# Three norms' rows turned by products with a diagonal, two early GpSimd steps, fewer idle products, and one wait moved, in a kernel of three transformer blocks

## The reference, cut to what matters

```python
def rmsnorm(x, g):
    y = x * lax.rsqrt(jnp.mean(x * x, axis=-1, keepdims=True) + EPS)
    return y * g

h = x                                               # block 1
h = h + token_mixer(rmsnorm(h, norm_mix), ...)      # two kinds of attention
h = h + hierarchical_moe(rmsnorm(h, norm_ffn), ...) # 32 experts of width 512
# blocks 2 and 3, l = 0 and 1
m = silu(c) @ w_ada[l] + b_ada[l]                   # six vectors: shifts, scales, gates
x = x + g_m * mixer(modulate(x, ...))               # l=0: attention with a context and a Fourier part; l=1: convolution
x = x + g_f * ec_moe(modulate(x, ...))              # 16 experts of width 1024, 32 rows each
```

## Time and profile before

| what | value |
|---|---|
| median of 3 runs | 1843.66 us (1841.27 to 1847.12) |
| the profiled execution, its own time | 1841.28 us |
| its span, first to last instruction | 1839.4 us |
| TensorE, VectorE, ScalarE, GpSimd busy | 77%, 27%, 13%, 5% of the span |
| data moved | 719 MB, 391 GB/s on average |
| first block's mixer | 0 to about 184 us |
| first mixture of experts | to about 640 us |
| second block's mixer | to about 830 us |
| its experts | to about 1260 us |
| third block's mixer | to about 1405 us |
| its experts and the end | to 1839.4 us |

### The profile page before, as it was taken

How to read it: one execution, slowest core, us unless ns; L and a number is a source line. 1 busy time by engine, 2 the same in 40 slices (tenths; PEclk the granted TensorE clock), 3 DMA queues, 4 the chain that set the end, 5 groups by cost and what they waited for, 6 DMA issues and landing times.

```text
span 1839.4 us, 30498 instructions
## 1 busy us (share of the span) xinstructions
PE 1419.1 (77%) x13602; PEld 818.7 (45%) x13602; DVE 488.9 (27%) x999; ACT 246.0 (13%) x561; POOL 83.1 (5%) x92
## 2 busy tenths in 40 slices
PE   9999886676588999999566666668999756666675
PEld 5456443333244454666233334326866433333332
DVE  5874221111221169841000000004643100000000
ACT  3233211111211113411000000001001000000000
POOL 3100000000000042100000000000000000000000
PEclk9999988888899999999777768789999877878888
DMA  9775999999999996788999999999998999999997
GB/s 366 261 291 236 386 428 427 426 427 425 426 421 422 402 340 245 296 355 368 431 431 429 430 431 431 426 427 390 392 379 332 429 432 432 428 431 431 431 423 323
DMA packets 79232, 719.28 MB, mean 391 GB/s; under 512 B 5104, under 2 KB 11000, under 8 KB 49656
## 3 DMA queue, kind: packets, MB, share of 16 engines
q1 hardware_dynamic: 76336, 712.85, 93.3%
q10 hardware_dynamic: 2760, 4.40, 0.7%
HBM read 716.18 MB, written 1.06 MB: 390 GB/s over the span
## 4 chain that ended last, share of the span: by engine, by line
DMA 50%; PE 38%; DVE 6%; issue 2%; POOL 2%; ACT 1%; SPq 0%; ACTq 0%; DVEq 0%
DMA ring<-in_moe_w_down 33%; PE bank L1792 9%; DMA ring<-in_w_down 8%; PE bank L2685 5%; PE bank L535 3%; DMA ring<-in_attn_w_in 3%; PE bank L1734 3%; DMA ring<-in_moe_w_gate 2%; PE bank L1743 2%; PE bank L1047 2%; PE bank L1016 2%; PE bank L679 2%; DMA room<-in_rows 1%; PE bank L2445 1%; PE bank L1646 1%
## 5 line engine op out<-in xcount | busy, mean ns | idle before, releaser
L1743 PE MATMUL bank<-ring,arena 128*32 128x256 f32 x3840 | 284.4, 460 | 165.4 <-DMA ring<-in_moe_w_up 123.6
L1792 PE MATMUL bank<-ring,arena 128*32 128x256 f32 x2944 | 236.1, 482 | 143.0 <-DMA ring<-in_moe_w_down 115.9
L1743 PEld LDWEIGHTS bank<-ring,arena 128*32 128x32 f32 x3840 | 159.1, 131 | 286.7 <-issue 219.7
L1792 PEld LDWEIGHTS bank<-ring,arena 128*32 128x32 f32 x2944 | 122.1, 136 | 244.8 <-issue 193.6
L1734 PE MATMUL bank<-ring,arena 128*32 128x512 f32 x976 | 130.5, 656 | 61.2 <-ACT arena L1834 32.0
L1865 DVE TENSOR_TENSOR arena<-arena,bank 128x128 f32<-128x128 f32 (+1 forms) x64 | 22.7, 354 | 503.9 <-PE bank L1743 496.5
L535 PE MATMUL bank<-ring,low 128*128 128x512 f32 (+1 forms) x352 | 150.9, 576 | 0.1
L1820 PE MATMUL bank<-arena 32*128 32x256 f32 x1024 | 92.6, 431 | 15.1 <-PE bank L1820 10.6
L1876 ACT ACTIVATE arena<-bank 128x256 f32<-128x256 f32 x64 | 24.6, 385 | 560.3 <-PE bank L1806 558.2
L535 PEld LDWEIGHTS bank<-ring,low 128*128 128x128 f32 x352 | 64.4, 190 | 64.3 <-issue 63.4
L1734 PEld LDWEIGHTS bank<-ring,arena 128*32 128x32 f32 x976 | 27.3, 114 | 140.3 <-issue 60.3
(11 more groups left out here) (322 smaller groups left out, 1336.5 us busy)
## 6 DMA issues: line engine op xcount, KB each, us to landing
ring<-in_moe_w_gate SPq DMA_DIRECT2D x20, 4096.0 KB, 24.4
ring<-in_moe_w_up SPq DMA_DIRECT2D x20, 4096.0 KB, 23.6
ring<-in_moe_w_down SPq DMA_DIRECT2D x20, 4096.0 KB, 23.7
ring<-in_w_gate SPq DMA_DIRECT2D x31, 2048.0 KB, 22.4
ring<-in_w_up SPq DMA_DIRECT2D x30, 2048.0 KB, 23.6
ring<-in_w_down SPq DMA_DIRECT2D x30, 2048.0 KB, 24.5
ring<-in_ada_w SPq DMA_DIRECT2D x24, 2048.0 KB, 13.7
ring<-in_moe_w_up SPq DMA_DIRECT2D x22, 2048.0 KB, 20.7
```

The source lines that it names most:

```text
L1743: last = nc.tensor.matmul(GU[up][32 * j:32 * j + 32, 0:QW], xgT[:, x + kk, a:a + C], w[:, kq, j * QW:(j + 1) * QW], start=(kk == 0), stop= ...
L1792: last = nc.tensor.matmul(z_bank(M)[32 * j:32 * j + 32, 0:QW], act_s[:, kk, :], w[:, kq, j * QW:(j + 1) * QW], start=(kk == 0), stop=(kk = ...
```

## The change

Four edits are made together.

- In the norms 0, 2 and 4 the rows are not scaled any more. ScalarE and VectorE scale the 128x128 identity by the roots instead, into the first 128 columns of the tile that held the squares, and `tr_pe` multiplies each raw 128x128 tile by that diagonal in place of the transpose. In norm 0 both engines also wait for the transfer of the identity.
- `FILL`: entry 4 from 25 to 22, entry 5 from 22 to 13, entry 9 from 9 to 6.
- `up_pe` of the first mixture no longer waits for ScalarE's copy of the gate sums; the gate's stacking products (`sums_pe` with up = 0) do.
- GpSimd gets two small steps between the norms 3 and 4, behind a wait for the last expert's down sums of the second block. Their results are read by nobody.

```diff
-FILL = (8, 5, 5, 25, 25, 22, 12, 7, 4, 9)
+FILL = (8, 5, 5, 25, 22, 13, 12, 7, 4, 6)
...
             act.wait_ge(norm_roots[0], j + 1)
-            nc.scalar.activation(dst[:, 0, :], src[:, 0, :], ACT.Copy, scale=rs[:, 0:1]).then_inc(xn_done[0], 1)
+            if j == 0:
+                act.wait_ge(first_loaded, 32)
+            nc.scalar.activation(dst[:, 0, 0:P], ident, ACT.Copy, scale=rs[:, 0:1]).then_inc(xn_done[0], 1)
...
             dve.wait_ge(norm_roots[1], j + 1)
-            nc.vector.tensor_scalar(dst[:, 1, :], src[:, 1, :], rs[:, 1:2], None, ALU.mult).then_inc(xn_done[1], 1)
+            if j == 0:
+                dve.wait_ge(first_loaded, 32)
+            nc.vector.tensor_scalar(dst[:, 1, 0:P], ident, rs[:, 1:2], None, ALU.mult).then_inc(xn_done[1], 1)
...
                 for kk in range(4 * b, 4 * b + 4):
-                    tile = (h if i % 2 else xn)[:, t, kk * P:(kk + 1) * P] if i else h[:, t, kk::KD]
-                    last = nc.tensor.transpose(banks[b][:, kk % 4 * P:(kk % 4 + 1) * P], tile, ident)
+                    tile = h[:, t, kk * P:(kk + 1) * P] if i else xn[:, t, kk::KD]
+                    dst = banks[b][:, kk % 4 * P:(kk % 4 + 1) * P]
+                    if i % 2:
+                        last = nc.tensor.transpose(dst, tile, ident)
+                    else:
+                        last = nc.tensor.matmul(dst, tile, (xn if i else h)[:, t, 0:P], start=True, stop=True)
...
         def up_pe(M, k, e, r):
             pe = nc.tensor
-            if M.nf == 1:
-                pe.wait_ge(M.g_act, nth(M, e + 1, 1, r, k))
-            elif e:
+            if e and M.nf == 2:
                 pe.wait_ge(M.act, nth(M, e, 1, r, k))
...
             if up:
                 pe.wait_ge(M.u_dve, nth(M, e + 1, 1, r, k))
-            elif M is M1 and so_far(CTX_TURN, e):
-                pe.wait_ge(ctx_dve, so_far(CTX_TURN, e))
+            else:
+                pe.wait_ge(M.g_act, nth(M, e + 1, 1, r, k))
+                if M is M1 and so_far(CTX_TURN, e):
+                    pe.wait_ge(ctx_dve, so_far(CTX_TURN, e))
...
             norm_pool(3)
+            pool.wait_ge(M2[0].z, E2)
+            nc.gpsimd.tensor_scalar(small[:, 213:214], zero_col[:, 0:1], 1.0, None, ALU.add)
+            nc.gpsimd.tensor_tensor(small[:, 214:215], const("ones")[:, 0:1], minus_half[:, 0:1], ALU.pow)
             norm_pool(4)
```

More of the change, by code:

```diff
@@ L1753, in sums_pe @@
                 pe.wait_ge(M.u_dve, nth(M, e + 1, 1, r, k))
-            elif M is M1 and so_far(CTX_TURN, e):
-                pe.wait_ge(ctx_dve, so_far(CTX_TURN, e))
[L1756 to L1759, removed]
+            else:
+                pe.wait_ge(M.g_act, nth(M, e + 1, 1, r, k))
+                if M is M1 and so_far(CTX_TURN, e):
+                    pe.wait_ge(ctx_dve, so_far(CTX_TURN, e))
+                    if so_far(UNITS, e):
+                        pe.wait_ge(cu_copied, T * so_far(UNITS, e))
+                    if so_far(UNIT_TURN, e):
+                        pe.wait_ge(cu_put, so_far(UNIT_TURN, e))
             src = up_s if up else gate_s
```

## The result

The changed kernel takes 1846.45 us (median of 12 runs, 1845.22 to 1849.57) against 1844.51 us for the kernel before (median of 12, 1841.27 to 1847.12). The ratio is 1.0017 with a 95% interval of 1.0009 to 1.0024, so the change costs 1.7 to 4.4 us. The two medians lie only 1.94 us apart (1.0011), which the interval holds as well. A second series of the same kernel gave 1.0017 again (1.0008 to 1.0027). The forecast was 0.95 us faster; the kernel is slower, by some 3 us after the ratio. That is inside the 0.3% that were called no change, but the interval leaves out both 1 and the forecast.

What follows compares the result with a forecast made beforehand. Weights stream at the ceiling except where no ring slot is free, so compute counts only at restarts. Terms +0.35 - 3.3 + 1.75 + 0.25 + 0 = -0.95 us, from 1843.66 to 1842.7 us; range 1839 to 1847.

Steps and rivals of the forecast that it cites:

- The start: First head: 16 turns cost 1.73 us more, fewer idle products save 0.65; +0.35 us passed on (0 to 0.5).
- the cover: First head: VectorE's idle wait for the second block's first conditioning weights absorbs 0.75 us of the 1.1 us delay.
- The moved wait: First expert stage: up products start earlier, ending the stream's stall near 225 us sooner; -3.3 us (-2.9 to -3.3).
- Rival 2: First expert stage: dropping the up products' wait brings nothing, another wait holding the transfer; +2.35 us, 1846.0; chance 0.1.
- The second block's turns: Second block: products with a diagonal take longer than transposes on TensorE, nothing absorbs it; +1.75 us (+1.7 to +2.1).
- rival 3: Second block: its turns are hidden behind VectorE, the busy engine in its middle; -2.7 us, 1841.0; chance 0.1.
- The third head: Third block's head: earlier diagonal but longer products, ScalarE's evictions held by its queued transfers; +0.25 us (0 to +0.7).
- The GpSimd steps: Before the third head: two early steps cost and gain 0, since GpSimd's long step there waits for VectorE's squares.
- rival 1: Third head: GpSimd was cold, so its step falls from 1.22 to 0.23 us; -1.95 us in all, 1841.7; chance 0.12.
- Rival 4: Third head: the clock falls to 1.2 GHz after TensorE idles; +4.5 us in all, 1848.2; chance 0.08.
- The arithmetic of restarts: Whole kernel: compute time counts only where it decides when a stopped weight stream starts again; no size of its own.

Runs made afterwards that it cites:

- late squares: Kernel before with the moved wait and VectorE's third-head squares waiting for the first tile's root; rows scaled and transposed 0.9975, with the diagonal 0.9974.

## Why the prediction was wrong

**The start is the step that failed.** The prediction said that "16 turns cost 16 x 0.108 = 1.73 us more" and that 0.35 us of the head's delay would be passed on (0 to 0.5). The turns cost 5.84 us more (7.78 against 1.94), and 4.4 us were passed on. The term of the sum that was mis-sized is the price of a record. It was taken from the earlier trace rows, whose weights lie one beside another, while the raw rows are read with a step of eight floats. A strided record measured 7.78 / 32 = 0.24 us, a contiguous one in the same place 3.73 / 32 = 0.117. Two runs bear it out from either side: the start alone has the root at 48.80, the changed kernel without it at 44.08. The diff states the step, `xn[:, t, kk::KD]`, and the trace of before had a hint. This is the view of its transposing line at the start, from scaled rows with the same step, and then in the second block, where the tiles are contiguous:

```profile
L377 PEld LDWEIGHTS bank<-room,h x16: 185/192/194, 8.5 to 10.2; 128*128 128x128 f32 x16
```

```profile
L377 PEld LDWEIGHTS bank<-room,low x16: 139/142/144, 652.0 to 657.4; 128*128 128x128 f32 x16
```

The transpose's load pays 50 ns for the step, and none of it shows: 16 took 1.94 us with the step and 1.97 without it. The product's load pays 144 ns, of which 127 show in each record (7.78 - 3.73 = 4.05 us in 32), twice per tile. Why it shows for the one and not for the other was not tested. Nobody would have got 144 out of 50, but a bound above 1.73 us was called for.

The Trainium skill (Advanced Engine Details and Errata, Memory Cachelines: SBUF Cachelines) says that SBUF has lines of 16 bytes, and that accesses which go to a different line each time are penalised. The trace agrees in direction, 192 to 336 ns at a step of 32 bytes. The page gives no price for a weight load.

The other half of that step, the cover, held. VectorE's wait of 0.75 us is gone from the changed kernel, the projection started 5.30 us late and 4.65 were passed on. Where the turns are contiguous the head's delay of about 1.6 us (projection at 12.57, against 11.00) passed on 0.9 us. With a contiguous step the term would have been +0.9 instead of +0.35, above its bound of 0.5. The three idle products, priced at 0.65 us, came out near that: the turns begin at 8.08 us in the mean of the four profiles with 22 and at 8.82 in that of the eight with 25, with a scatter of over 1 us in each group.

**The moved wait** was right in place, mechanism and size: -3.1 us by stretch C against -3.3, 1.73 us for a group against 1.74, the stall gone. By the whole, alone, it gave 4.1 us (the interval, 0.9966 to 0.9987 of 1843.59 us, is 2.4 to 6.3 us less). Rival 2 is refuted.

**The second block's turns** were right: +1.82 us against +1.75. Nothing hid them, so rival 3 is refuted for this stretch; that the whole pays them in full was not shown.

**The third head** was right in every step and low in size: +0.56 against +0.25, inside its bounds, mostly because a record took 0.12 us and not 0.108 (3.84 us for the turns, against 3.46). ScalarE's queue bound its evictions as said.

**The GpSimd steps** gain nothing, as said, and rival 1 is refuted: the head's step stays at 1.21 us after work 2.85 us earlier, and falls to 0.22 us when VectorE is silent. The Trainium skill (SBUF — State Buffer, SBUF: two separate sides) calls the port pair an exclusive lock for a whole instruction; the kernels with late squares agree with it.

**Rival 4** is refuted in both profiles of the changed kernel: the turns took 3.84 us, 0.12 a record, and the granted clock was 1.00 in every window of 4 us from 1262 to 1282.

**What hid the error.** The arithmetic of restarts held: alone, the start cost 2.6 to 6.3 us of the whole and the moved wait gave 2.4 to 6.3. Because the two nearly cancel, a term wrong by 4 us moved the whole by 0.2%. That the measured 1846.45 us still lies in the forecast's range of 1839 to 1847 is luck: the measured stretches on the 1843.66 us that the forecast started from give 1847.4.

**What stays open.** Two more stretches vary: from the second block's first root to the chain's first wait for weights behind it (846.59 us in the kernel before), and from the third projection to the end. Their sum is 749.7 to 750.6 us in the seven kernels without a diagonal in the second block and 750.6 to 752.1 in the five with one, 0.95 us more in the mean. The rows of the chain account for most of this difference. The 16 products near 745 us took 4.42 to 5.14 us instead of 3.46 in seven of the twelve profiles, four of them with that diagonal; 14 idle products took 2.79 instead of 1.56 us in one, and 50 took 6.92 instead of 5.58 in another, both with it. Where only the 16 products were slow the sum is 750.4 to 750.6 without the diagonal and 750.6 to 750.7 with it, so the turns bring no further cost that the chain shows.

The 32 gather products at the start of the two later expert stages vary as well. The chain of the kernel before:

```profile
826.67 5.47 PE bank L1646 x32
...
1402.12 3.84 PE bank L1646 x32
```

and of the kernel with only the second block's turns:

```profile
829.38 3.84 PE bank L1664 x32
...
1403.33 5.47 PE bank L1664 x32
```

The granted clock is down to 0.54 over the slow gather of the second kernel (1406 to 1408 us). All seven profiles without that diagonal, and the first of the changed kernel, have the first pattern; the other four with it have the second. So the turns of the second block may shift where the clock falls, here with no net effect on the sum. Whether they also make it fall more often, or chance does, twelve profiles don't settle, and no run held it apart.

## What to carry to other kernels

Price a product by the nearest row of the same layout, not only the same shape: a step in the stationary operand's tile is a cost of its own, and a row of the same step, even of another operation, is a warning. Replacing a pass over the rows by products pays only where that pass ends the wait and the products behind it cost less than it did; at none of the three heads was that so, and with late squares too the scaled and transposed rows had the shorter head (8.30 against 8.79 us), though that pair also differs in the transfers' place and the idle products. The parts of a change should be timed apart: what gains here is the moved wait (0.9977 of the time before). Late squares, with the transfers moved, shorten the third head by another 0.8 us in the trace, which the time of the whole (0.9975) can't confirm.

## What the hardware showed that was not expected

- A weight load of 128x128 float32 took 336 ns where neighbouring weights lie eight floats apart, and 192 ns where they touch; for transposes it took 192 and 142 ns. The 32 product records took 7.78 us with the step and 3.73 without it.
- A two-input pass of VectorE (1.23 us) held a one-column step of GpSimd at 1.14 to 1.22 us at every head where they overlapped; without overlap it took 0.22 us after 444 and after 448 us idle.
- The clock is at 1.2 GHz over a batch of idle products in some executions and not in others (2.73 to 5.23 us for the same 24). Two executions of one kernel differed by 3.1 us at its first gather products (183.59 and 186.70), 2.5 of them in this batch.
- The same 32 gather products took 3.84 or 5.47 us, and in each of the twelve profiles exactly one of the two later expert stages had the slow ones.
